# The filler matmuls between the output projection and the experts, left out

## What is computed

```python
def reference(x, ...):
    h = x
    h = h + token_mixer(rmsnorm(h, norm_mix_w[0]), w_in[0], ..., w_branch[0], w_out[0])
    h = h + moe_ffn(rmsnorm(h, norm_ffn_w[0]), w_router[0], b_router[0], w_mlp1[0], b_mlp1[0], w_mlp2[0], b_mlp2[0])
    return rmsnorm(h, norm_final_w)

def moe_ffn(xn, ...):
    logits = (xt @ w_router + b_router)              # 256 x 32
    top_val, top_idx = lax.top_k(logits, 4)
    gate = jax.nn.softmax(top_val, axis=-1)
    # per expert e, on the tokens that chose it:
    hdn = xb @ w_mlp1[e] + b_mlp1[e]                 # 1024 -> 2048
    glu, lin = clamp(hdn[:, :1024]), clamp(hdn[:, 1024:])
    act = glu * sigmoid(1.702 * glu) * (lin + 1.0)
    y = act @ w_mlp2[e] + b_mlp2[e]                  # 1024 -> 1024, then times gate, summed per token
```

## Time and profile before

| | us |
|---|---|
| median of 3 executions | 1146.25 (1146.23 to 1148.27) |
| the profiled execution | 1146.16 |
| its span, first to last instruction | 1144.4 |
| PE busy | 1083.5 |
| DVE busy | 367.8 |
| ACT busy | 240.4 |

### The profile page before, as it was taken

How to read it: one execution, slowest core, us unless ns; L and a number is a source line. 1 busy time by engine, 2 the same in 40 slices (tenths; PEclk the granted TensorE clock), 3 DMA queues, 4 the chain that set the end, 5 groups by cost and what they waited for, 6 DMA issues and landing times.

```text
span 1144.4 us, 14875 instructions
## 1 busy us (share of the span) xinstructions
PE 1083.5 (95%) x5415; PEld 492.4 (43%) x5416; DVE 367.8 (32%) x786; ACT 240.4 (21%) x332; POOL 3.6 (0%) x12
## 2 busy tenths in 40 slices
PE   9999999799999999999999999999999999999996
PEld 8888878533333333333333333333333333333332
DVE  6977787522222222222222222222211112222223
ACT  4845673211111111111111111111111111111112
POOL 1000000000000000000000000000000000000000
PEclk9999999999999999999999999999999999999998
DMA  9654466999999999999999999999999999999994
GB/s 339 213 170 161 147 196 249 426 429 426 428 428 428 430 427 430 428 430 427 428 429 429 428 428 428 429 428 428 429 428 430 427 430 428 430 427 428 428 428 184
DMA packets 45199, 439.57 MB, mean 384 GB/s; under 512 B 6044, under 2 KB 6232, under 8 KB 20504
## 3 DMA queue, kind: packets, MB, share of 16 engines
q1 hardware_dynamic: 43344, 436.68, 91.5%
q10 hardware_dynamic: 1832, 2.55, 0.7%
HBM read 438.17 MB, written 1.05 MB: 384 GB/s over the span
## 4 chain that ended last, share of the span: by engine, by line
PE 62%; DMA 33%; DVE 2%; ACT 2%; issue 1%; SPq 0%; DVEq 0%; ACTq 0%
PE bank L981 21%; DMA late_slots<-in_w_mlp_dram 18%; DMA ring<-in_w_mlp_dram 15%; PE bank L1007 15%; PE bank L669 9%; PE bank L902 4%; PE bank L941 2%; PE bank L663 2%; PE bank L862 2%; PE bank L838 2%; PE bank L925 1%; ACT sgm L583 1%; PE bank L917 1%; PE bank L968 1%; DVE rlo L1063 0%
## 5 line engine op out<-in xcount | busy, mean ns | idle before, releaser
L981 PE MATMUL bank<-ring,sga 128*64 128x512 f32 x1264 | 282.0, 594 | 23.0 <-DMA ring<-in_w_mlp_dram 23.0
L981 PE MATMUL bank<-late_slots,sga 128*64 128x512 f32 x848 | 190.1, 594 | 16.6 <-DMA late_slots<-in_w_mlp_dram 16.6
L981 PEld LDWEIGHTS bank<-ring,sga 128*64 128x64 f32 x1264 | 89.7, 136 | 202.1 <-issue 151.4
L1007 PE MATMUL bank<-ring,sgm 128*64 128x512 f32 x656 | 146.4, 595 | 0.0
L1472 DVE TENSOR_SCALAR sga<-bank 128x512 f32<-128x512 f32 x33 | 22.8, 692 | 334.0 <-PE bank L981 334.0
L981 PEld LDWEIGHTS bank<-late_slots,sga 128*64 128x64 f32 x848 | 59.4, 136 | 138.1 <-issue 100.9
L590 ACT ACTIVATE sgm<-bank 128x512 f32<-128x512 f32 x33 | 19.8, 600 | 455.1 <-PE bank L981 455.1
L1492 DVE SCALAR_TENSOR_TENSOR moe_y_lo<-bank,st,moe_y_hi 128x512 fp32r<-128x512 f32 x33 | 24.8, 751 | 237.2 <-ACT moe_y_hi L597 237.2
L1007 PE MATMUL bank<-late_slots,sgm 128*64 128x512 f32 x400 | 89.7, 595 | 0.0
L1007 PEld LDWEIGHTS bank<-ring,sgm 128*64 128x64 f32 x656 | 45.2, 137 | 84.8 <-issue 82.3
L597 ACT ACTIVATE moe_y_hi<-bank,st 128x512 fp32r<-128x512 f32 x33 | 22.7, 688 | 259.4 <-PE bank L1007 259.4
(11 more groups left out here) (264 smaller groups left out, 869.6 us busy)
## 6 DMA issues: line engine op xcount, KB each, us to landing
ring<-in_w_mlp_dram SPq DMA_DIRECT2D x116, 2048.0 KB, 37.1
late_slots<-in_w_mlp_dram SPq DMA_DIRECT2D x76, 2048.0 KB, 37.5
ring<-in_w_in_dram SPq DMA_DIRECT2D x22, 1024.0 KB, 5.1
ring<-in_w_branch_dram SPq DMA_DIRECT2D x4, 1024.0 KB, 4.9
ring<-in_w_out_dram SPq DMA_DIRECT2D x4, 1024.0 KB, 6.5
xs<-in_x_dram SPq DMA_DIRECT2D x2, 512.0 KB, 3.8
out_dram<-xn ACTq DMA_DIRECT2D x2, 512.0 KB, 2.6
xn<-in_b_mlp_dram ACTq DMA_DIRECT2D x3, 256.0 KB, 7.9
```

The lines of the kernel that those rows point to most:

```text
L981: last = mm(B[4 + u][g * C:(g + 1) * C, :], xgT[:, k % 4, k // 4, :], places[at[k // 2]][:, k % 2, u * FF + g * N:u * FF + (g + 1) * N], s ...
L1007: last = mm(B[7][g * C:(g + 1) * C, :], actT[:, j, h * C:(h + 1) * C], places[at[4 + h]][:, j // 2, (j % 2) * D + g * N:(j % 2) * D + (g + ...
```

## The change

The four calls of `keep_warm` in and around the router go, and with them the name `tables`. The call at the start of the kernel stays. Lines below them move up by two to six.

```diff
@@ def _(pe): (PE's list)
             mm = nc.tensor.matmul
 
-            tables = cst[:, K_MASK:K_MASK + S]
-
             def keep_warm(n, table):
...
             pe.wait_ge(mgT_ready, 4)
             turn_tile(0)
-            keep_warm(5, tables)
             turn_tile(1)
...
             last.then_inc(logits_done, 1)
-            keep_warm(3, tables)
             pe.wait_ge(chosen, 1)
...
-            keep_warm(3, tables)
             pe.wait_ge(pos_ready, 1)
             gather(2)
 
             turn_router_gates(2)
             turn_rows(1)
-            keep_warm(3, tables)
             pe.wait_ge(b2_in, 32)
```

## The result

The changed kernel takes 1150.18 us (median of 11, 1149.41 to 1152.05) against 1146.25 us: a ratio of 1.0033, 95% interval 1.0024 to 1.0042. It is slower by 3.9 us, with the interval clear of 1. The forecast was 1147.4 us and its range ended at 1150.0 us. The profiled execution took 1150.57 us with a span of 1148.8 us, 4.4 us over that of before. In this execution two thirds of the 4.4 us are what the prediction was about, and the rest was lost ahead of the router, most of it near 42 us, where the diff touches nothing.

A forecast was written before the change was run, and what follows sets the result against it. The expert load stream was taken as the bound: 5.1 us of delay to the first release less 3.9 us of margin stops it for 1.2 us, nothing saved elsewhere, so 1146.16 + 1.2 = 1147.4 us; range 1145.8 to 1150.0 us.

The forecast's parts named there:

- What bounds the kernel: From 186 to 1115 us the unbroken stream of expert weight loads at 428 GB/s sets the end; PE has room.
- The fillers' own time, 0: Removing the 14 filler matmuls between 205 and 225 us saves 0, since PE's next starts wait for other things.
- the chain's 1.30 us: Fourth filler group's share of the chain before the experts' first matmul; at most 1.30 us saved; rival with it on path 2%.
- The clock falls in the router: Without fillers, gaps of up to 3.1 us drop PE to half clock somewhere in the router; forecast case, 38%.
- the early version: Variant with PE's clock already low at 209.5 us, before the second tile's transposes; 1148.3 us, chance 25%.
- The price, 5.1 us of delay: Half clock delays the first release of a place: 3.0 us in the router plus 2.05 us in the first tile.
- The margin of 3.9 us: The eleventh expert load, issued at 229.4 us, could come 11.2 - 7.3 = 3.9 us later before the stream stops.
- The one sign named for a wrong margin: The load issue at 229.4 us moving by over 5 us while the kernel's end doesn't move.
- The early-fall rival: Transposes before the router's matmuls don't hold the clock, so it is low at 209.5 us; 1148.3 us (1146.3 to 1150.4), 25%.
- The long low clock: Half clock lasts through the first expert tile's four places, some 14 us; end at 1159.4 us, chance 5%.

The follow-up runs named there:

- after_again: The changed kernel itself, run once more with nothing altered for another profiled execution; ratio 1.0033 against the kernel before.
- delay_22: The kernel before with 22 matmuls instead of 3 in the fourth filler group, behind the turned rows; median 1150.76 us, ratio 1.0036.

## Why the prediction was wrong

- **What bounds the kernel: right.** 428 GB/s from 240 to 1115 us, and the end moves with the stream in every row of the table.
- **The fillers' own time, 0: right for time saved.** The bias starts no earlier without group 4. The sequencer's register loads were the right row to go by, and the chain's 1.30 us was not on the path.
- **The clock falls in the router: right.** Named as the likeliest, with and without the early version 63%.
- **The price, 5.1 us of delay (3.0 in the router, 2.05 in the first tile): right in size.** Measured 4.75 us (3.2 and 1.6) and 5.71 us (4.0 and 1.7) in two executions. The sum was a middle between two places of the fall, and the two executions came to lie at either side of it, which is in part luck. The gather was put at 3.7 us and took 3.68.
- **The margin of 3.9 us: wrong, and this is the step that put the forecast out.** It was the difference of two landing times. The runs show 1.9 us. The forecast was 2.8 us too low. With 1.9 us in the prediction's own sum, 5.1 - 1.9 = 3.2 us, 1149.4 us, so the margin accounts for 2.0 us of the miss. With the delay of after_again, 5.7 - 1.9 = 3.8 us, 1150.0 us; the last 0.2 us, and how many executions were late by that much, stay open. The margin was used as exact, and the range had no bound for it; its two ends should have been the 3.9 us of the landing times and 0. The one sign named for a wrong margin (an issue late by over 5 us with no move of the end) looked only for a margin that was too small.
- **The early-fall rival** came nearest in time (1148.3 us, up to 1150.4 us) and the place of its fall (209.5 us) was right in after_again, but its reason (transposes) was wrong.
- **The long low clock** did not happen: the clock was back 3.2 us (after_again: 4.0 us) behind the start of the bias; without group 4 it took 6.2 us. Its sum also mixed two lengths: the 3.4 us are about what 16 records of a place take, while from the bias to the release it was 4.23 us.
- **Not seen at all:** that the clock comes back behind the gather and falls a second time around the register loads, whose gap the fourth group covers; and that before itself has two groups of times.

## What to carry to other kernels

A stretch in which PE waits for others is harmless in a load-bound kernel only as long as the buffers behind it come free in time: look for the first release after the stretch and how long the load queue lasts from there. Measure that margin by the rate of the queue, and take a delay by some filler work of known length to find where the end begins to move; landing times overstated it here. Cheap work that keeps PE's clock up in the gaps was worth 3.9 us here, though none of it was on any path.

## What the runs showed of the hardware

- A queue of 2 MB loads lost stream well before its last load had landed: in delay_22 the rate fell 27.1 us behind the output projection and the last load landed at 29.2 us. The next load had to be issued by about 25.6 us (the 23.75 us of before and the free 1.9 us): issued 3.02 us later than in before, 1.2 us of stream were lost, and 1.60 us later, 0.2 us.
- The clock fell without any gap of PE, 1.3 us behind 2.2 us of matmuls on four rows (42.3 us), in one execution of the changed kernel and not in the other. That these matmuls are the reason is not shown.
- It stayed up through 5.9 us in which PE did transposes alone, with gaps of under 0.9 us.
- After its return behind the gather it fell again at 230.0 us, at the end of a gap of 2.7 us of PE, and came back at 233.4 us, with PE at work since 230.2 us. In after_again the second fall came at 229.9 us, when PE had been at work again since 229.2 us.
